# Two-layer hybrid encoder, eight cores: first projection through SyncE in fp32, expert-weight conversions in quarters, new DMA numbers in the list scheduler

## The reference

```python
h = x
for layer in range(2):
    y = rmsnorm(h, norm_mix_g[layer])
    y = pool_attn_mixer(y, ...) if layer == 0 else sgu_mixer(y, ...)
    h = h + y
    h = h + hier_moe(rmsnorm(h, norm_ffn_g[layer]), ...)
return rmsnorm(h, final_norm_g)
```

## Time and profile before

| | us |
|---|---|
| median of 3 runs | 1968.24 (1963.76 to 1993.67) |
| the profiled execution | 1961.25 |
| its span on the slowest core (core 4), first to last instruction | 1959.5 |
| its other cores | 1902.4 to 1948.0 |
| PE busy on core 4 | 1626.9 (83%) |
| DVE / ACT / POOL busy | 1108.7 (57%) / 858.7 (44%) / 669.9 (34%) |
| mean granted PE clock on core 4 | 0.929 |

### The profile page before, as it was taken

How to read it: one execution, slowest core, us unless ns; L and a number is a source line. 1 busy time by engine, 2 the same in 40 slices (tenths; PEclk the granted TensorE clock), 3 DMA queues, 4 the chain that set the end, 5 groups by cost and what they waited for, 6 DMA issues and landing times. The chain is left out here.

```text
span 1959.5 us, 29742 instructions; the slowest of 8 cores (1902.4 to 1959.5 us)
## 1 busy us (share of the span) xinstructions
PE 1626.9 (83%) x10480; PEld 810.3 (41%) x10480; DVE 1108.7 (57%) x2459; ACT 858.7 (44%) x1364; POOL 669.9 (34%) x884
## 2 busy tenths in 40 slices
PE   2789898998999669999965979888999548879896
PEld 1334444353454334444432545444545224334442
DVE  1545564665655645555543656565566356656674
ACT  2445555556666323333324545534554124434452
POOL 2244441342332442323311133333333244334432
PEclk9899899899999879999997989888999769999998
DMA  9855779569535455578754776576659936564520
GB/s 219 168 103 131 109 143 189 81 158 156 121 101 190 134 174 190 189 241 220 206 132 158 162 161 117 127 177 162 135 122 224 230 140 200 170 210 168 171 95 36
DMA packets 92790, 309.64 MB, mean 158 GB/s; under 512 B 15016, under 2 KB 27688, under 8 KB 88416
## 3 DMA queue, kind: packets, MB, share of 16 engines
q0 software_dynamic: 53808, 147.39, 35.8%
q1 hardware_dynamic: 38832, 160.23, 26.8%
HBM read 407.25 MB, written 137.49 MB: 278 GB/s over the span
## 5 line engine op out<-in xcount | busy, mean ns | idle before, releaser
L653 PE MATMUL psum<-arena 128*128 128x512 bf16 x3072 | 716.5, 386 | 13.5 <-ACT arena L641 7.8
L653 PEld LDWEIGHTS psum<-arena 128*128 128x128 bf16 x3072 | 298.3, 100 | 366.2 <-issue 31.1
L641 ACT ACTIVATE arena<-psum 128x512 f32<-128x512 f32 (+3 forms) x471 | 302.7, 673 | 333.1 <-PE psum L653 127.7
L967 PE MATMUL psum<-arena 128*128 x1536 | 376.9, 385 | 28.6 <-ACT arena L641 23.0
L634 POOL TENSOR_SCALAR arena<-arena 128x1 f32<-128x1 f32 x208 | 62.7, 301 | 540.7 <-ACT arena L712 243.8
L967 PEld LDWEIGHTS psum<-arena 128*128 128x128 bf16 x1536 | 150.4, 99 | 212.7 <-issue 59.5
L970 ACT ACTIVATE arena<-psum 128x256 f32<-128x256 f32 x192 | 73.1, 381 | 299.1 <-PE psum L967 298.8
L990 PE MATMUL psum<-arena 128*128 x768 | 197.9, 388 | 0.2
L935 POOL DMA_INDIRECT arena<-H,arena x96 | 105.0, 1093 | 222.9 <-DMA H<-arena 102.8
L994 DVE TENSOR_TENSOR arena<-psum,arena 128x1024 f32<-128x1024 f32 x96 | 117.4, 1223 | 94.8 <-PE psum L990 94.8
L641 DVE COPY arena<-psum 128x256 bf16<-128x256 bf16 (+3 forms) x186 | 69.6, 375 | 162.2 <-PE psum L978 79.0
(11 more groups left out here) (162 smaller groups left out, 1880.8 us busy)
## 6 DMA issues: line engine op xcount, KB each, us to landing
arena<-WB SPq DMA_DIRECT2D x100, 1536.0 KB, 12.8
WB<-wmoe POOLq DMA_DIRECT2D x32, 1536.0 KB, 27.6
arena<-x SPq DMA_DIRECT2D x64, 512.0 KB, 9.0
H<-arena SPq DMA_DIRECT2D x64, 512.0 KB, 10.2
arena<-H SPq DMA_DIRECT2D x64, 512.0 KB, 12.1
arena<-ab_w_in POOLq DMA_DIRECT2D x4, 1024.0 KB, 38.8
arena<-sgu_w_in POOLq DMA_DIRECT2D x4, 1024.0 KB, 12.8
TBL<-arena SPq DMA_DIRECT2D x2, 1536.0 KB, 14.5
```

Of the source, the lines that this page charges most:

```text
L641: fs = {"act": lambda e: e.activation(out=dst, in_=g(), func=AF.Copy), "dve": lambda e: e.tensor_copy(dst, g()), "pool": lambda e: e.tenso ...
L653: P.add("pe", lambda e, kc=kc: e.matmul(bank(b), lhsT=lhs(kc), rhs=rhs(kc), start=(kc == 0), stop=(kc == n - 1)), reads=reads(kc), writes= ...
L967: return e.matmul(bank(b), lhsT=tT[i % 2][:, kc, :], rhs=wslice(e, i, x_, kc * 1024), start=(kc == 0), stop=(kc == 7))
```

## The change

The arithmetic is the same; what moves is who loads, who rounds and when DMAs are issued.

- **Start.** `ab_w_in` comes as fp32 (2 MB per quarter) through SP into staging buffers that later hold other tiles, and is rounded to bf16 by 16 copies of 128x1024 (`cast_w`) which the scheduler shares between ACT and DVE: 14 on ACT and 2 on DVE. SP's issues of the first strip are chained in recorded order (`P.chain`): x block 0, gM, ident, x block 1, the first weight quarter, x 2 and 3, the other three quarters, x 4 and 5, then the remaining constants, the four `load_r`, and x 6 to 8. `identb` is a copy on DVE instead of a DMA.
- **Conversions.** Each expert is converted by four DMAs of 32 rows (128 POOL DMAs in all, before 32). `conv_some`, called at each step of the strips' generators with that step's count, records one quarter for every 28 counts in layer 0 (from the second strip on) and every 30 in layer 1; each waits for the last recorded PE operation. What is left over is recorded before the expert loads.
- **Scheduler.** Landing is taken as 3000 ns (`LAND`), for stores 7000 ns (`LAND_OUT`, not for a moe's last four scatters); the rates are 130 shared, 200 on POOL, 270 on SP.
- **Expert loads.** Layer 0: four before the last `out0`, two after the last `load_r`. Layer 1: two before the last `out1`, four one by one with its steps.

```diff
+LAND = 3000.0
+LAND_OUT = 7000.0
...
+        if self.chain is not None and eng == "sync":
+            op.order.update(self.chain[-1:]); self.chain.append(op)
...
-                half = min(op.lat, max(0.0, ot - t0) * 120.0)
-                dma_t[e] = t0 + half / 120.0 + (op.lat - half) / (240.0 if e == "pool" else 200.0)
-                op.fin = dma_t[e] + 2000.0
+                half = min(op.lat, max(0.0, ot - t0) * 130.0)
+                dma_t[e] = t0 + half / 130.0 + (op.lat - half) / (200.0 if e == "pool" else 270.0)
+                op.fin = dma_t[e] + op.land
...
-        def convert(l, e_, extra):
+        def convert(l, e_, q, grp, extra):
-            r = slice((l * 16 + e_) * 128, (l * 16 + e_ + 1) * 128)
+            r = slice((l * 16 + e_) * 128 + q * 32, (l * 16 + e_) * 128 + q * 32 + 32)
             P.add("pool", lambda e: e.dma_start(out=WB[r, :], in_=wmoe[r, :], max_dma_last_dim=8192),
-                  writes=[("wb", l, e_)], grp=P.group("cv%d_%d" % (l, e_)), extra=extra, t=(1000, 3100000))
+                  writes=[("wb", l, e_)], grp=grp, extra=extra, t=(1000, 780000))
...
                 P.add("sync", lambda e: e.dma_start(out=self.dst[blk * 128:(blk + 1) * 128, :], in_=xr), reads=[kx], writes=[("dst", l, blk)],
-                      grp=P.group("st%d" % i))
+                      grp=P.group("st%d" % i), land=LAND_OUT)
...
-                      reads=["gidx", k("hr", h)], writes=[("sc", l, i)], grp=P.group("hs%d" % h))
+                      reads=["gidx", k("hr", h)], writes=[("sc", l, i)], grp=P.group("hs%d" % h), land=LAND_OUT if i < NM - 4 else LAND)
...
-        for q in (1, 2, 3, 0):
-            load_cols(w_in[:, q], ab_w_in.rearrange("(kc p) n -> p kc n", p=128)[:, :, q * 512:(q + 1) * 512], ("Awin", q))
+        stg = []
+        for q, o in enumerate((R2 + 52 * K1, R2, R1 + 52 * K1, R2 + 36 * K1)):
+            P.at(("stg", q), o, 16 * K1); stg.append(view(o, [128, 8, 512]))
+        def load_w(q):
+            P.add("sync", lambda e: e.dma_start(out=stg[q], in_=ab_w_in.rearrange("(kc p) n -> p kc n", p=128)[:, :, q * 512:(q + 1) * 512]), writes=[("stg", q)], grp=P.group("w_%d" % q))
+        def cast_w(q):
+            for h in range(4):
+                copy(w_in[:, q, 2 * h:2 * h + 2, :].rearrange("p a b -> p (a b)"), stg[q][:, 2 * h:2 * h + 2, :].rearrange("p a b -> p (a b)"), [("stg", q)], [("Awin", q)], ("act", "dve"))
...
+        pace = {"left": [], "acc": 0, "step": 1 << 30, "grp": None}
+        def conv_start(l, step):
+            pace.update(left=[(l, e_, q) for e_ in range(16) for q in range(4)], acc=0, step=step)
+        def conv_some(n):
+            pace["acc"] += n
+            while pace["left"] and pace["acc"] >= pace["step"]:
+                pace["acc"] -= pace["step"]
+                l, e_, q = pace["left"].pop(0)
+                if q == 0:
+                    pace["grp"] = P.group("cv%d_%d" % (l, e_))
+                convert(l, e_, q, pace["grp"], [next(o for o in reversed(P.all) if o.eng == "pe")])
         def run_all(*gens):
             for g in gens:
-                for _ in g:
-                    pass
+                for n in g:
+                    conv_some(n)
...
+                if s == 0 and c == 1:
+                    for q in (2, 3, 0):
+                        load_w(q)
                 yield next(g)
+            if s == 0:
+                for q in (1, 2, 3, 0):
+                    cast_w(q)
+                const_rest(); poolw_load()
+                for i in range(M0.nr):
+                    M0.load_r(i)
...
-        M0.load_x(0); M0.load_x(1)
-        for i in range(M0.nr):
-            M0.load_r(i)
+        M0.load_x(0); start_loads(); M0.load_x(1)
+        P.add("dve", lambda e: e.tensor_copy(identb, ident), reads=["ident"], writes=["identb"])
+        load_w(1)
         run_all(stage1n(0))
+        P.chain = None
...
-                convs(0, 1, P.all[-1])
...
-                convs(0, 2, P.all[-1])
+                if s == 0:
+                    conv_start(0, 28)
+        conv_some(1 << 30 if pace["left"] else 0)
...
-        for i in range(NSLOT):
+        for i in range(4):
             expert_load(0, i, (R1, i), wk0[i])
         run_all(out0(NS - 1))
+        for i in range(4, NSLOT):
+            expert_load(0, i, (R1, i), wk0[i], after=[M0.last_r])
...
+        conv_start(1, 30)
         for s in range(NS):
             run_all(norms1(s), vstage(s), ustage(s))
-            convs(1, 2, P.all[-1])
...
-        for i in range(NSLOT):
+        conv_some(1 << 30 if pace["left"] else 0)
+        for i in range(2):
             expert_load(1, i, (R2, i), wk1[i])
-        run_all(out1(NS - 1))
+        g = out1(NS - 1); n = 2
+        for _ in g:
+            if n < NSLOT:
+                expert_load(1, n, (R2, n), wk1[n], [P.all[-1]]); n += 1
```

39 lines of the change are left out of this document (18 added, 21 removed).

## The result

The changed kernel takes 1877.28 us (median; 1867.63 for the profiled execution), the kernel before 1966.0 in the same comparison: 0.9545 of the time, 95% interval 0.9478 to 0.9613. A second comparison, run beside the experiments, gave 0.9483 (0.9432 to 0.9534). So it is faster, by about 5%; forecast were 1861 us. The profiled execution is 93.6 us shorter than that of before (1867.63 against 1961.25; from first to last instruction 1865.7 against 1959.5).

What follows compares the result with a forecast made beforehand. PE sets the pace but is kept waiting, mainly by late loads and by gathers waiting for scatters. Terms -16 - 9 - 40 - 10 + 3 - 17 - 18 = -107 gave 1854, forecast 1861 us as median; range 1820 to 1930.

Steps and rivals of the forecast that it cites:

- Start, -16 forecast: Start: x block 7 no longer waits behind other loads, so the second strip's projections begin near 75.5 us, not 91.3.
- Until then the DMA engines are full: Start of the kernel before: DMA was taken as full until the second strip's projections at 91.3 us (share 1.07 and 1.15).
- Gap at 143.8, rest of the attention strips and late pieces, -16 together: Attention strips: -9 for PE's gap at 143.8 us, -10 for other idle time, +3 for layer 0's last conversion pieces.
- Layer 1, -40: Layer-1 strips: conversions in quarters remove three quarters of five PE gaps' 43.95 us (-33), and slow clock (-7).
- 6 to 9 us from issue to use: Layer-1 strips: estimated x load time when meeting one or two quarters, against 7.4 us that cost PE nothing.
- rival 1: Strips: spread conversions are nearly always in flight, x loads still land in about 11 us, gaps stay; 1920 us, chance 0.15.
- rival 4: Whole kernel: the new order opens new waits as large as those it closes; 1955 us, chance 0.08.
- Expert loads, -17: End of layer 1: two instead of five expert loads precede the last residual rows, which move up 17 us, ending a 16.15 us wait.
- Second mixture, -18: Second mixture: planning 7000 ns for scatter landing moves gathers later, mostly ending 18 waits (66.5 us); bounds 0 to -34.
- First mixture, 0: First mixture: no term; it has the same gathers but no norm on POOL, and was said to lose little.
- Rival 2: Conversions: quarters' fixed time holds the DMA engines, layer-1 strips run full and attention strips get gaps; 1940 us, chance 0.04.
- Rival 3: POOL's queue: quarters waiting for PE hold up the roots behind them, making the kernel slower; 2045 us, chance 0.05.

Runs made afterwards that it cites:

- a_bunch: Changed kernel with quarters kept but issued eight at once, two experts at the old places, instead of at an even pace: 0.9700 of the time before.
- a_whole: Changed kernel with each expert's conversion as one whole piece at the same even pace, instead of four quarters: 0.9584 of the time before.
- a_model: Changed kernel with the scheduler's old numbers (2000 ns to land for all, rates 120, 240 and 200): 0.9690 of the time before.
- c_after: The changed kernel again, unaltered, run beside the experiments as their common base: 0.9483 of the time before.
- i_moe: Changed kernel with 16 of layer 1's 64 quarters issued during the first mixture, the rest every 40 counts, layer 0 every 25: 0.9560 of the time before.
- i_x2: Changed kernel with x-load landing planned as 16000 ns in layer 1, 7000 in layer 0, and layer-0 quarters every 25 counts: 0.9586 of the time before.

## Why the prediction was right, and where it was not

The forecast lay 16 us under the first median, on the right side and in its range, by terms that miss in both directions; that they nearly cancel is luck. Of the 94 us, 15 are the slowest core coming nearer to the mean, which no term has. Undone one at a time, the pace costs 43 us, the scheduler's numbers 41, the expert loads 4 and the start 3: 91 of the 102 that the change gained in the second comparison (0.0517 x 1980), though what is undone alone need not add up. Term by term, on the mean over the cores:

- *Start, -16 forecast: -4, and none of it by the loads.* The bytes came as worked out: the windows of the first 70 us of the changed kernel add up to 18.5 MB, at 264 GB/s on the mean. (The Trainium skill's 358 GB/s, beside which the prediction sets its 275, stands in the page "SBUF — State Buffer" under "Summary: rules for kernel authors", not in the section that it names.) Two steps failed. "Until then the DMA engines are full" is not so in the kernel before: their share from 70 to 80 us is 0.02, and x block 7 was in SBUF at 62.8, 28 us ahead of the projections at 91.3; earlier bytes for it could win nothing by themselves. And "from a landed x block to its copy in SBUF it takes 5.5 us" is a row taken where POOL and DVE were idle; block 7 arrives in the middle of the first strip's pooling, where 12 us pass from its sum of squares at 73.36 to the projections at 85.48. What sets this time in both kernels is the first strip's work on ACT, POOL and DVE, which no term asked about.
- *Gap at 143.8, rest of the attention strips and late pieces, -16 together: -20.* The mechanism is right: x loads there land in 5.5 instead of 13.3 us, and with the bursts back (a_bunch) in 14.4. It is the even pace that does this; whole pieces at that pace (a_whole) come as early and lose their time at the strips' end instead. The scheduler's numbers, which have no term here, hold 10 of the 20 us (a_model). The late pieces cost about what was said: the dispatch's wait at the end of layer 0 is 13.80 us against 8.85 in the kernel before.
- *Layer 1, -40: -11 (c_after -4).* The old gaps went, as forecast, but nothing sure was won. The step that failed is "6 to 9 us from issue to use", against 7.4 that are free: 60% of the loads land later than 7.4 us in both executions of the changed kernel, 48% did before, and where ACT waits for one, 15 us pass from its issue to its use. As rival 1 said, the spread quarters are in flight nearly always there; nor do they stay evenly spread: at the gap of 24.29 us POOL, which waits for PE with each, let three go at once. The wait moved from the residual add to the router, as rival 4 had it, and a_bunch moves it back at the same length of the stretch. What sets that length stays open: i_moe, with a quarter fewer bytes beside these loads, is the only run clearly below the rest, and there 45% of the loads land later than 7.4 us; but in a_whole, on the four cores that show it, 46% do, and its stretch is 418.0.
- *Expert loads, -17: -15, by another cause.* The step "these move up by 3 x 1.6 MB" is wrong as the cause: with the loads back in place 2 to 3 us return, with the conversions back in bursts 15. The right size was luck.
- *Second mixture, -18: -32.* Mechanism right, size not. Over the whole stage PE's idle time fell by 22.9 us (56.7 to 33.8) and its busy time by 9.2, at a granted clock of 0.970 instead of 0.947: near the 21.6 of idle time and 13 of slow clock that the prediction works out and of which it then takes only 18. And the step gave 7000 ns all the credit, where the first 1000 ns and the rates already bring 24 us.
- *First mixture, 0: +3 and 0* in the two executions, right.

Of the rivals, 1 nearly describes the loads of layer 1, and nothing else. Rival 2 has its sign there, a DMA share near 0.9, but at the same pace quarters cost only 0.3 to 1.0 us per MB more than whole pieces, on the whole less than the pace does. The rule of the Trainium skill that spoke for it ("DMA: Bandwidth & Descriptors", section "Bandwidth", transfers of 1 MiB and more) finds only a small price in these runs: at the even pace 7.7 us per MB for pieces of 1.5 MB and 8.0 to 8.3 for quarters. Rival 3 did not come for the conversions, though POOL's queue is part of what the start lost to. Rival 4, a gain given back at new lines, is the router's gap.

Of the signs that the prediction names, two came: no 16 us wait behind the expert loads, and gathers that wait 3.1 us in all. The others did not: the second strip's projections came at 85.5 us, not 75, the x loads of layer 1 in 9 us and more, the DMA share there was 0.85, old gaps were left on two cores, and the mean granted clock was 0.950.

## What to carry to other kernels

A burst of background transfers shows as the same gap in every period. Spreading it paid here in a stage with a DMA share of 0.64, and only moved the wait in one with 0.70, which it raised to 0.85; so look at the bytes beside the loads, and at who else needs them, before counting gaps as gains. Where an order is planned from estimates, one that is a few microseconds short can put a waiting instruction ahead of everything on its queue: later landings are the cheapest edit here and brought two fifths of the mean core's gain (32 of 79 us), and one raised too far (i_x2) cost 30 us in its stage. Before a term is built on bytes that arrive earlier, look up in the trace of before when the block in question landed and when it was used; and take the time from arrival to use at the place where the arrival will fall.

## What was unexpected of the hardware

The DMA share of a stretch is a poor measure of the room left in it, for the same bytes can fill it more or less: in layer 1 the conversions took 6.1 us of the 16 engines per MB in bursts of whole pieces and 8.0 to 8.3 as quarters at an even pace (means over the cores), and the share of the stretch rose from 0.70 to 0.85 on the profiled cores, for 22.1 and 24.4 MB of them. And the same edit brought x loads in after 4.8 to 5.0 us instead of 13.4 in the attention strips, but after 9.0 to 10.3 instead of 7.0 in layer 1; why the two stages differ is not shown. The spread of the cores, 57 us before, fell to 29 us with the change, without any edit to what one core does differently from another; why is open.
